# Two stacked experts and a combination summed on TensorE, in a two-layer decoder kernel

## What is computed

```python
def hier_moe(h, ln_g, w_gr, b_gr, w_er, b_er, w1, w3, w2):
...
    xf = rms_norm(h, ln_g).reshape(n, c)
...
    ew, ei = lax.top_k(jax.nn.softmax(el, axis=-1), MOE_TOPK)
    weight = grp_w * ew / jnp.sum(ew, -1, keepdims=True)
    expert = grp * MOE_EXPERTS_PER_GROUP + ei
...
    def expert_block(args):
        xb, e = args
        return (jax.nn.silu(xb @ w1[e]) * (xb @ w3[e])) @ w2[e]

    yb = lax.map(expert_block, (xbuf, blk_e)).reshape(p, c)
    y = jnp.zeros((n, c), yb.dtype).at[buf_t].add(yb * buf_w[:, None].astype(yb.dtype))
    return y.reshape(bt, t, c)
...
        lc = (jnp.einsum('bghqd,bgkd->bghqk', qc, k_cmp).astype(f32) * scale
              + table[:, :, rel_bucket(tq[:, None] - cmp_end[None, :])])
        pc = masked_softmax(lc, cmp_end[None, :] <= tq[:, None])
        oc = jnp.einsum('bghqk,bgkd->bghqd', pc.astype(v_cmp.dtype), v_cmp)
```

## Time and profile before

| | |
|---|---|
| runs | 1943.08, 1943.29, 1943.59 us; median 1943.29 |
| profiled execution | 1943.08 us, of which the span from first to last instruction 1941.3 us |
| TensorE busy | 1815.1 us, 94% of the span |
| VectorE, ScalarE, GpSimd busy | 595.7, 358.9, 217.7 us |
| granted clock of TensorE, mean | 0.959 |
| DMA | 499.73 MB, 257 GB/s over the span |

### The profile page before, as it was taken

One profiled execution on the slowest core, in us unless ns is written; L12 is line 12 of the kernel. 1 busy time (PEld: TensorE's weight loads), 2 busy tenths in 40 slices (PEclk: granted clock), 3 DMA queues, 4 the chain that ended last, 5 costly groups with the idle time before them and its releaser, 6 DMA issues.

```text
span 1941.3 us, 25898 instructions
## 1 busy us (share of the span) xinstructions
PE 1815.1 (94%) x11066; PEld 959.5 (49%) x11066; DVE 595.7 (31%) x1273; ACT 358.9 (18%) x842; POOL 217.7 (11%) x263
## 2 busy tenths in 40 slices
PE   7979988989799999999969998999979999999993
PEld 3334347755554454445444576555554444454440
DVE  5463793452221111111040434564122111111113
ACT  1442113311100000000030113665110000000001
POOL 1044000000000000000020001454000000000002
PEclk9989998999799999999969999999979999999997
DMA  5111743060899999999969202010379999999994
GB/s 206 52 78 42 278 123 52 3 268 1 345 414 430 428 427 432 430 428 429 418 233 155 62 22 109 13 30 5 130 289 407 427 432 428 431 427 430 429 402 151
DMA packets 60930, 499.73 MB, mean 257 GB/s; under 512 B 28079, under 2 KB 28591, under 8 KB 42383
## 3 DMA queue, kind: packets, MB, share of 16 engines
q1 hardware_dynamic: 53391, 481.26, 62.1%
q0 software_dynamic: 7424, 16.80, 2.4%
HBM read 465.23 MB, written 41.18 MB: 261 GB/s over the span
## 4 chain that ended last, share of the span: by engine, by line
PE 84%; DVE 8%; issue 3%; DMA 2%; POOL 1%; ACT 1%; SPq 0%; POOLq 0%; DVEq 0%
PE bank L1397 71%; PE bank L1449 5%; PE bank L1985 3%; PE bank L1999 2%; DVE spare L1008 2%; DVE arena L1009 1%; PE bank L1785 1%; DVE arena L1260 1%; DMA arena<-y_rows,ints 1%; POOL arena L493 1%; DMA arena<-gram_dram 1%; PE bank L1405 1%; POOL arena L491 0%; DVE arena L1022 0%; PE bank L1557 0%
## 5 line engine op out<-in xcount | busy, mean ns | idle before, releaser
L1397 PE MATMUL bank<-arena 128*64 128x512 f32 (+10 forms) x5202 | 1258.8, 540 | 25.3 <-DVE arena L973 9.5
L1397 PEld LDWEIGHTS bank<-arena 128*64 128x64 f32 (+5 forms) x5202 | 485.2, 156 | 675.9 <-issue 653.0
L1397 PEld LDWEIGHTS bank<-const,arena 128*128 128x128 f32 x2048 | 238.2, 195 | 51.2 <-issue 48.7
L1397 PE MATMUL bank<-const,arena 128*128 128x128 f32 x2048 | 250.0, 281 | 2.2 <-DVE const L1139 2.2
L513 POOL DMA_INDIRECT y_rows<-arena,ints x64 | 63.0, 985 | 1124.3 <-ACT arena L749 909.5
L1214 DVE TENSOR_TENSOR arena<-arena,bank 128x256 f32<-128x256 f32 x64 | 26.9, 421 | 426.5 <-ACT arena L743 426.5
L749 ACT ACTIVATE arena<-bank 128x512 f32<-128x512 f32 x64 | 38.2, 597 | 424.3 <-PE bank L1397 424.3
L743 ACT ACTIVATE arena<-bank 128x256 f32<-128x256 f32 x64 | 24.5, 383 | 468.6 <-PE bank L1397 468.6
L1146 DVE TENSOR_TENSOR arena<-bank,vec 128x512 f32<-128x512 f32 x64 | 44.3, 691 | 192.7 <-PE bank L1397 192.7
L559 POOL TENSOR_SCALAR arena<-arena,small 128x128 f32<-128x128 f32 (+3 forms) x128 | 76.5, 607 | 150.6 <-DVE small L1374 150.6
L1223 DVE COPY arena<-bank 128x256 f32<-128x256 f32 x64 | 27.1, 424 | 184.3 <-PE bank L1785 184.3
(11 more groups left out here) (238 smaller groups left out, 980.7 us busy)
## 6 DMA issues: line engine op xcount, KB each, us to landing
arena<-m_w SPq DMA_DIRECT2D x64, 4096.0 KB, 18.5
arena<-m_w SPq DMA_DIRECT2D x64, 2048.0 KB, 16.5
y_rows<-state SPq DMA_DIRECT2D x1, 8192.0 KB, 22.6
arena<-kv_w SPq DMA_DIRECT2D x1, 6144.0 KB, 18.3
rev_bias<-arena SPq DMA_DIRECT2D x1, 5120.0 KB, 69.7
arena<-a_wk SPq DMA_DIRECT2D x2, 2048.0 KB, 14.9
arena<-a_wr SPq DMA_DIRECT2D x2, 2048.0 KB, 7.9
arena<-a_wv SPq DMA_DIRECT2D x2, 2048.0 KB, 8.0
```

Of the source, the lines that this page charges most:

```text
L1397: return nc.tensor.matmul(dst, lhsT, rhs, start=start, stop=stop)
```

## The change

- Start: the one-hot matrices are loaded first, on ScalarE's queue. TensorE makes the tables from 4 matmuls ahead of the first transposes, VectorE evacuates them ahead of the first norm step, and they are kept as 16 rows in DRAM. `bias_c` is loaded from there later, and the skewed table is made there from DRAM to DRAM.
- Experts 30 and 31 (`EARLY` = 30) are no longer stored. Their results go to rows 0 to 63 (expert 30) and 64 to 127 (expert 31) of banks 6 and 7, and stay in SBUF. The rows of the other 30 are gathered as soon as expert 29's store has landed.
- TensorE sums all: for each block j of tokens, 4 matmuls with weights that are diagonal (a token's weight on the diagonal, 0 for the last two experts) over the gathered rows, and 2 with `tail_T` (a one-hot matrix times the weight, transposed by TensorE) over the stacked results. VectorE adds the sums to h. New on VectorE: the making of these matrices (`tail_picks`) and nine small steps in `entries`.
- Compressed branch: values in 8 matmuls of 128 weights' columns, scores in 8 matmuls a block against keys of two heads laid on a diagonal (`kcmp_diag`), every block in a bank of its own, ScalarE's last exponential ahead of the copy of unit 10.
- Regions are dealt out anew (w_qg, w_kv, keys, values, probs), w_kv is loaded in three parts, and w_qg's two parts later.

Tiles:

```diff
+        tail_T = const[:, one_hot_at + 512:one_hot_at + 1024].rearrange("p (j t) -> p j t", j=NJ)
+        early_diag = region(2)[:, 2048:3072].rearrange("p (n t) -> p n t", n=2 * NJ)
```

SyncE:

```diff
+            sp.wait_ge(sem("bias_ev"), 4)
+            sp.dma_start(bias_dram, bias_rows).then_inc(sem("bias_out"), 16)
             sp.wait_ge(sem("tr_done"), NK)
...
-            sp.wait_ge(sem("hidden_mm"), at("hidden_mm", E - 2))
-            sp.dma_start(w_qg[:, 0:7, :], d["b_wqg"][:, 0:7, :]).then_inc(sem("q_w_in"), 16)
-            sp.wait_ge(sem("expert_mm"), at("expert_mm", E - 2))
-            for i in range(2):
-                sp.dma_start(fwd[i], d["bucket_fwd"]).then_inc(sem("bias_in"), 16)
...
-            sp.dma_start(w_qg[:, 7, :], d["b_wqg"][:, 7, :]).then_inc(sem("q_w_in"), 16)
+            sp.wait_ge(sem("hidden_mm"), at("hidden_mm", E - 1))
+            sp.dma_start(w_qg[:, 0:4, :], d["b_wqg"][:, 0:4, :]).then_inc(sem("q_w_in"), 16)
+            sp.wait_ge(sem("y_got1"), at("y_got1", 32))
+            sp.wait_ge(sem("expert_mm"), at("expert_mm", E - 1))
+            sp.dma_start(w_qg[:, 4:NK, :], d["b_wqg"][:, 4:NK, :]).then_inc(sem("q_w_in"), 16)
             overflow_sp(0)
             sp.wait_ge(sem("combined"), 8)
-            sp.dma_start(w_kv, d["kv_w"]).then_inc(sem("kv_w_in"), 16)
+            for i in range(3):
+                sp.dma_start(w_kv[i], d["kv_w"][:, i, :, :]).then_inc(sem("kv_w_in"), 16)
+            for a in range(8):
+                sp.dma_start(bias_c[16 * a:16 * a + 16, :, :],
+                             bass.AP(tensor=bias_dram.tensor, offset=9 - a, ap=[[64, 16], [1664, NH], [1, NOFF]])
+                             ).then_inc(sem("bias_c_in"), 16)
...
-            sp.wait_ge(sem("rev_ev"), at("rev_ev", 1))
-            sp.dma_start(rev_dram, spread(rev_rows, 1, P)).then_inc(sem("rev_out"), 16)
+            sp.dma_start(rev_dram, spread(bias_dram[:, 1024:1664], 1, P)).then_inc(sem("rev_out"), 16)
```

GpSimd, in `moe_pool`:

```diff
-                for e in range(E):
+                for e in range(EARLY):
...
+                for i in range(2):
+                    pool.wait_ge(sem(f"y_store{i}"), 16 * (EARLY // 2) * (l + 1))
+                pool.wait_ge(sem("hidden_mm"), at("hidden_mm", E * l + EARLY))
+                for j in range(NJ):
+                    for c in range(2):
+                        nc.gpsimd.indirect_dma_start(
+                            out=y_got[:, j, c, :], out_offset=None, in_=y_rows,
+                            in_offset=bass.IndirectOffsetOnAxis(ap=slot_i[:, j, c:c + 1], axis=0)
+                        ).then_inc(sem(f"y_got{j}"), 16)
```

ScalarE:

```diff
+            nc.scalar.dma_start(fwd, d["bucket_fwd"]).then_inc(sem("bucket_in"), 16)
+            nc.scalar.dma_start(rev, d["bucket_rev"]).then_inc(sem("bucket_in"), 16)
+            nc.scalar.dma_start(rel[0:32, :], d["rel_bias"]).then_inc(sem("bucket_in"), 16)
...
             cmp_turned(1)
+            cmp_exp(3)
             kv_out_act(10)
-            cmp_exp(3)
```

VectorE:

```diff
+            nc.vector.memset(rel[32:33, :], NEG).then_inc(sem("rel_mask"), 1)
+            dve.wait_ge(sem("bias_mm"), 1)
+            for i in range(2):
+                nc.vector.tensor_copy(bias_rows[:, 512 * i:512 * i + 512], bank[4 + i][0:NH, :]).then_inc(sem("bias_ev"), 1)
+            nc.vector.tensor_scalar(bias_rows[:, 1024:1536], bank[6][0:NH, :], -1.0, None, ALU.mult).then_inc(sem("bias_ev"), 1)
+            nc.vector.tensor_scalar(bias_rows[:, 1536:1664], bank[7][0:NH, 0:128], -1.0, None, ALU.mult).then_inc(sem("bias_ev"), 1)
             for j in range(NJ + 1):
...
             def combine(l, j):
-                dve.wait_ge(sem(f"y_got{j}"), 32 * (l + 1))
-                for c in range(2):
...
-                    nc.vector.scalar_tensor_tensor(h[:, j, :], y_got[:, j, c, :], combine_w[:, j, c:c + 1], h[:, j, :],
-                                                   ALU.mult, ALU.add).then_inc(sem("combined"), 1)
+                dve.wait_ge(sem("tail_out"), at("tail_out", NJ * l + j + 1))
+                for q in range(2):
+                    cols = slice(512 * q, 512 * q + 512)
+                    nc.vector.tensor_tensor(h[:, j, cols], bank[2 * j + q][:, :], h[:, j, cols],
+                                            ALU.add).then_inc(sem("combined"), 1)
```

TensorE:

```diff
+            pe.wait_ge(sem("bucket_in"), 48)
+            pe.wait_ge(sem("rel_mask"), 1)
+            for i in range(2):
+                mm(bank[4 + i][0:NH, :], rel, fwd[:, 512 * i:512 * i + 512])
+            mm(bank[6][0:NH, :], rel, rev[:, 0:512])
+            mm(bank[7][0:NH, 0:128], rel, rev[:, 512:640]).then_inc(sem("bias_mm"), 1)
             pe.wait_ge(sem("ident_in"), 16)
...
+                def apart(slot):
+                    return [bank[6 + slot][CAP * q:CAP * q + CAP, :] for q in range(2)]
+
+                def stacked(slot):
+                    return [bank[6 + q][CAP * slot:CAP * slot + CAP, :] for q in range(2)]
+
+                def tail_turn():
+                    pe.wait_ge(sem("tail_hot"), at("tail_hot", l + 1))
+                    for j in range(NJ):
+                        last = nc.tensor.transpose(bank[2][:, P * j:P * j + P],
+                                                   one_hot[:, 0, j, :, :].rearrange("p e t -> p (e t)"), ident)
+                    last.then_inc(sem("tail_mm"), 1)
+
+                def early_part(j):
+                    pe.wait_ge(sem(f"y_got{j}"), at(f"y_got{j}", 32 * (l + 1)))
+                    for q in range(2):
+                        for c in range(2):
+                            mm(bank[2 * j + q][:, :], early_diag[:, 2 * j + c, :], y_got[:, j, c, 512 * q:512 * q + 512], c == 0, False)
+
+                def late_part(j):
+                    for q in range(2):
+                        last = mm(bank[2 * j + q][:, :], tail_T[:, j, :], yb[:, q, :], False, True)
+                    last.then_inc(sem("tail_out"), 1)
...
-                    result(n % 2, w_slot[n % 3][2].rearrange("p (k n) -> p k n", k=4), "expert_mm")
+                    result(stacked(n % 2) if e >= EARLY else apart(n % 2), hT[:, n % 2, :, :, :], w_slot[e % 3][2].rearrange("p (k n) -> p k n", k=4), "expert_mm")
...
+                    if e == EARLY:
+                        tail_turn()
...
+                early_part(0)
+                pe.wait_ge(sem("yb_ready"), at("yb_ready", E * (l + 1)))
+                late_part(0)
+                for j in range(1, NJ):
+                    early_part(j)
+                    late_part(j)
...
-            for m in range(NOFF):
-                mm(bank[m % 2][:, 16 * (m // 2):16 * (m // 2) + 16], fwd[m % 2][:, 864 - 16 * m:992 - 16 * m], rel[m % 2])
...
             def cmp_scores(j):
-                if j >= 2:
-                    pe.wait_ge(sem("cshifted"), at("cshifted", j - 1))
-                for hh in range(NH):
...
+                for m in range(NP):
+                    last = mm(bank[cmp_bank[j]][:, 64 * m:64 * m + 64], q_T[:, m, P * j:P * j + P],
+                              kcmp_diag[:, m // 2, :, :].rearrange("p i k -> p (i k)"))
                 last.then_inc(sem("cS_mm"), 1)
```

More of the change, by code:

```diff
@@ L28 @@
 SLOTS = (E + OVER) * CAP
+EARLY = E - 2
 NG, HPG, NH = 4, 4, 16
@@ L264, in decoder_program @@
[L264 to L266 removed]
+                for i, o in ((1, 0), (1, 2048), (8, 0), (8, 2048))]
+        values = region(9)[:, 0:2048].rearrange("p (j b n) -> p j b n", j=NJ, b=2)
+        kcmp_diag = region(9)[:, 3664:3920].rearrange("p (g i k) -> p g i k", g=NG, i=2)
+        gates = region(9)[:, 2832:3024].rearrange("p (j n) -> p j n", j=NJ)
@@ new lines, in decoder_program @@
+        bias_dram = nc.dram_tensor("bias_rows", (NH, 1664), FP32, kind="Internal").ap()
+        xT_b = region(5).rearrange("p (k t) -> p k t", k=NK)
+        q_T = region(3).rearrange("p (m t) -> p m t", m=NP)
+        cmp_w1 = [region(i).rearrange("p (m n) -> p m n", m=16) for i in (4, 7)]
+        blocks_in = [region(5)[:, o:o + 1984].rearrange("p (m g k) -> p m g k", m=16, g=NG) for o in (0, 2048)]
+        cmp_w2 = [small[:, 96:352].rearrange("p (s n) -> p s n", s=2), region(9)[:, 3024:3152].rearrange("p (s n) -> p s n", s=2)]
@@ L1312, in cmp_softmax @@
                     dve.wait_ge(sem("cT_mm"), at("cT_mm", j - 1))
-                for par in range(2):
-                    s = bank[cmp_bank(j, par)][:, 0:256].rearrange("p (h k) -> p h k", h=NH // 2)
-                    last = nc.vector.tensor_tensor(w[:, par::2, :], s[:, :, 0:NCMP], bias_c[:, par::2, lo:lo + NCMP], ALU.add)
-                then(last)
+                s = bank[cmp_bank[j]][:, :].rearrange("p (h k) -> p h k", h=NH)
+                then(nc.vector.tensor_tensor(w, s[:, :, 0:NCMP], bias_c[:, :, lo:lo + NCMP], ALU.add))
                 then(nc.vector.reduce_max(cmax, w, axis=AX.X))
@@ L2090, in by_row @@
         return w.reshape(-1, P, w.shape[1]).transpose(1, 0, 2)
-    for n in ("kv_w", "cmp_k_w1", "cmp_v_w1"):
+    for n in ("cmp_k_w1", "cmp_v_w1"):
         x[n] = by_row(a[n])
```

(1 more changed line is left out.)

265 lines of the change are left out of this document (147 added, 118 removed), and 2 rows, old and new, of the table GOES_ON.

## The result

The changed kernel takes 1950.18 us (median of 14 runs, 1947.68 to 1952.82), the kernel before 1943.28 on the same chip (14 runs). The ratio is 1.0036, with a 95% interval of 1.0026 to 1.0047: slower by about 7 us, of 8.0 forecast. The profiled execution took 1951.74, with a span of 1949.5 (before: 1941.3), so the traces differ by 8.2.

What follows compares the result with a forecast made beforehand. TensorE, busy 94% of the span, was taken to bound the kernel. Start +4.4, layer 0's seam +5.85, compressed branch -5.75 and layer 1's end +3.5 gave +8.0 on 1943.1: 1951.1 us, range 1940.5 to 1957.5.

Steps and rivals of the forecast that it cites:

- Start: Kernel start: loads, half-speed table matmuls and VectorE's evacuations ahead of the first norm step shift everything by +4.4 us (3 to 6).
- Rival D: The start's shift is absorbed by a load that ends last later on: +3.6 us, 1946.7; chance 0.05.
- Layer 0's seam: End of layer 0's experts to query projection: turn, slower stacked results, TensorE's sums and late turn blocks cost +5.85 us.
- order cost: Layer 0, sums to projection: turn blocks behind all sums, VectorE's evacuation ahead of its last add; 1007.4 to 1017.55.
- The stacked results at 6.9 us: Results of experts 30 and 31, both layers: one column half idle, 6.86 us against 3.6, so +3.25 each.
- Rival A: Stacked results run as fast as the paired ones, saving 3.25 us for each of four: 1938.1 us; chance 0.13.
- Compressed branch: Values, scores and ScalarE's last exponential moved ahead of unit 10's copy: -5.75 us in sum (-8.8 to -2.7).
- The exponential's part: Compressed branch: TensorE's wait before the last turn goes (-3.55 us), unit 11 runs without the clock's fall (-1.9).
- The clock's part: Compressed branch: today's clock loss in small matmuls kept (1.4 us unit 7, 1.65 unit 9); alternatives +3 or -3.05.
- Layer 1's end: Last expert stage to span end: turn, stacked results and 20.6 us of sums, ending at 1944.8: +3.5 us (3 to 5).
- Rival C: Position rows' DRAM-to-DRAM spread is slow, cmp_w1[1] queues behind it, TensorE waits 10 us: 1961; chance 0.07.
- Rival B: Clock holds in turn blocks (-2.65 us) and compressed branch (-3.05), loads land early (-1.4): 1944.0; chance 0.13.

Runs made afterwards that it cites:

- the control: The changed kernel itself, without an edit, run again on the chip of later experiments: 1949.97 us, ratio 1.0057 to the kernel before.
- the second experiment: Changed kernel with the tables' matmuls behind the first block transposes, evacuated on ScalarE, their store behind lora_g's load: 1943.09 us, ratio 1.0002 to the kernel before.
- the first experiment: Changed kernel with the result matmuls of experts 30 and 31 alternating between the column halves: 1938.98 us, ratio 0.998 to the kernel before.
- The runs with the better order: Changed kernel with each block's variance and scaling right behind its combination in layer 0, run twice: 1952.37 us (ratio 1.0053) and 1951.03 us (1.005).
- the keys' copies first: Changed kernel with the compressed keys' copies ahead of unit 6's on ScalarE, TensorE's wait for unit 6's moved later: 1945.05 us, ratio 1.001 to the kernel before.

## Why the prediction was right

The time (1951.1 forecast, 1950.18 measured) and the sign follow from the four terms, and in the profile first shown each is within 1 us of its forecast. That it is so close is in part luck. In the control's profile the seam with the clock behind it is +3.2 and the branch -4.5, each within its range and 1 to 3 us off, and the total there is +5.6 for 8.0. What was right is the mechanism: the stacked results that don't pair up, the tables ahead of the first transposes, and the exponential, each shown by an experiment of its own. Where the terms are off:

- **Start, +4.4 forecast, +4.8 measured.** The loads landed at 6.00, not 5.5 (and between 6.0 and 7.9 in other executions). The tables took 5.73 us, at half speed all the way: for 3.25 matmuls of 512 columns that is 1.76 each, where full speed gives 0.857. The sum had let the last 0.8 us run at full speed. The evacuations took 2.0 instead of 2.35. The first transposes stood at 15.26, not at about 14. The step on which it rested, to go by durations and not by the granted clock of 1.00 that the profile prints there, was right; by the printed clock the term would have been +2.4. The Trainium skill, "TensorE: Matmul & The Clock Gate", Part 1, says that the throttled state is the default, and the trace's 5.73 us for the first work of the engine agree with it. Rival D is out: the shift was still +4.8 at 966 us. And the term was a choice of place, as the second experiment shows.
- **Layer 0's seam, +5.85 forecast, +5.2 measured** to the first query matmul (10.0 less 4.8), and +0.8 more up to the values of the branch, with the clock at 0.50 until 1027. The last result was forecast at 986.8 + 4.8 = 991.6 and ended at 991.7. The sums, forecast at 20.6 us, took 20.7. The order cost was 9.3 us from last sum to projection, where 10.15 had been put (1007.4 to 1017.55). The stacked results at 6.9 us were the term that decided the sign, and the first experiment shows that their cause was read rightly from the gate's narrow matmuls. Rival A would have needed 3.6. Its turning point is wrong in the prediction: 8.0 us over four results are 2.0 each, so the sign turns where a stacked result takes under 6.9 - 2.0 = 4.9 us, and not under 5.6. The gathers began at 976.7, 6.1 us behind the store of expert 29 where some 3.3 had been put, and were hidden all the same. And the position-table matmuls of the kernel before took 9.4 us and not 7.6, which is the time of their weight loads; nothing in the sum hangs on it.
- **Order cost.** That about 2 us of it were VectorE's order was right; that they would be worth 2 us was not. The runs with the better order gained them and lost them to the clock right behind.
- **Compressed branch, -5.75 forecast, -6.2 measured.** The exponential's part, -5.45, is borne out alone in the kernel before (-5.5 in the trace), though unit 11 by its own two rows gives 1.7 of it and not 1.9. The clock's part was right in its sum and wrong in its reason. The text kept the loss of the small matmuls in both pairs of blocks: -0.3 for the first pair with the values, 0 for the second. The clock fell for 6 us in the first pair, which made it +1.3, and did not fall in the second (17.55 us at 1.00 for 19.46 before), which made it -1.9. That the two nearly cancel is luck; in the control the first pair is +2.9. Whether 64-column matmuls are too light was not the question: it was the gap of 0.94 us ahead of them. The text had ScalarE's copies in it only as the reason why the values gain no more than 0.3 us; the gap cost 4.5 us in this profile and 6.1 in the control's.
- **Layer 1's end, +3.5 forecast, +3.6 measured** (+3.5 in the control). The sums ran at full speed behind the stacked results, as the forecast had it.
- **Rival C** (the position rows' spread turns slow) was priced from the copy out of SBUF, and the new copy moved its bytes in less than half the time (about 20 us for 46).
- **Rival B** (1944.0) looked at the right resource, the clock, and its price for the branch (-3.05) was about what the keys' copies first brought beyond their gap (4.5 - 0.94 = 3.6). It takes an edit that the change does not make.

## What to carry to other kernels

Matmuls that fill half the columns were only cheap in pairs here (8 of them 3.65 us alternating, 6.9 us in one half): before results are stacked into one half of PSUM's rows, look for the matmul that runs beside them in the other half, or alternate two outputs. Hiding a gather behind TensorE's work pays what the wait was, less what that work costs; here the two were equal within 1.2 us over both layers by the trace. New work at the very start of a kernel should be tried behind the first thing on the chain and not ahead of it: here that gave back 4.1 us of 4.8. And a gap of under 1 us can cost more than itself where small matmuls follow it, as the 4.5 to 6.1 us behind a gap of 0.94 show. So the gain of a reordering is to be read in what follows the seam too, and not at the seam alone.

## What was not expected of the hardware

- The clock's fall is not the same from execution to execution of one kernel. Behind layer 0's sums it stood at 0.50 from 1017 to 1027 in one profile and from 1017 to 1020 in the other; in the scores from 1157 to 1163 and from 1154 to 1163.
- In the profile of the tables' experiment a stretch of full 128x512 matmuls ran at 0.54 (207 to 240 us, 38 records) that the changed kernel ran at 1.00 (72 records), with the same code there. What decides it stays open.
- A spread of 5120 KB from 16 rows landed 69.7 us after its issue out of SBUF and 21.6 after it from DRAM to DRAM. Some 22 of the 69.7 passed while earlier loads were still moving. After that the DMA engines were 95% busy at about 100 GB/s until 1076 us; the new copy moved at 331 to 401 GB/s from 1036 to 1056 with the engines about as busy. So other traffic does not explain the difference, but the two sources were not tried against each other with all else equal.
